# Eight modulation tiles moved from the first layer's FFN to the second layer's front units and mixers

## The chip, the cores and the metric

The kernel runs on one core of one Trainium2 chip. The metric is the device time of the whole program in microseconds (us), the median of several runs. The five engines of a core run their own instruction streams and meet at semaphores: TensorE (PE in the profile; its weight loads are PEld), VectorE (DVE), ScalarE (ACT), GpSimd (POOL) and SyncE (SP, which here only issues DMAs).

## The reference

One inference step of a trunk of two layers, for 128 context tokens and 256 latent tokens with 1024 channels. All is float32. Each layer, for each of the two groups of tokens, computes

```
sh1, sc1, g1, sh2, sc2, g2 = split(silu(c) @ w_mod + b_mod, 6)     # c of the latent group, c_ctx of the context
h   = rmsnorm(x, norm1_g) * (1 + sc1) + sh1
u, q, k, v, z, xbc, dt = split(h @ w_in)
three mixers: pooling of u; differential attention of q, k, v; bidirectional state-space scan of z, xbc, dt
gates = sigmoid(h @ w_gate + b_gate)
x   = x + g1 * ((sum of gate * (mixer @ w_branch)) @ w_out)
h2  = rmsnorm(x, norm2_g) * (1 + sc2) + sh2
up  = dwconv3(h2 @ ffn_w_up);  x = x + g2 * ((silu(up_gate) * up_value) @ ffn_w_down)
```

and a last RMSNorm follows. Context tokens see context tokens only; latent tokens see both. The change is about the first line: the 6 x 1024 values of modulation per layer and group.

## The kernel before

Both groups of tokens go through together as one block of T = 384 columns; activations lie transposed, channels on the 128 partitions. The work of a layer is a fixed list of 140 units (`UNITS`), most of them one tile of 128 output channels: 8 XBC, 4 UU, 4 QQ, 4 KK, 4 VV, 4 ZZ, 24 GATE, 12 BRANCH (two tiles each), 8 OUT, 44 UP, and 24 DOWN (8 tiles in three parts). Each engine walks through the same list in the same order, and its instructions wait for counts that the others reach.

A float32 product is made of three faster ones: weights and activations are split into a high part (rounded to the format fp32r) and a low part. For unit u+3, while unit u is in work (`AHEAD` = 3), ScalarE writes the high part `wh` of the weights (`hi`, L1155), VectorE the low part `wl` (`lo`, L1508), from `raw`, which SyncE loads, 512 KB a unit. TensorE then runs three matmuls for each block: L823, L824, L825. `wh` and `wl` have three buffers each.

The mixers' own work is spread over the units from ZZ to BRANCH: step s is done in unit `MIX0` + s (`MIX0` is the first ZZ, unit 24; GATE 0 is unit 28).

**Modulation.** For one tile of 128 modulation channels, VectorE multiplies a tile of `w_mod` (`rawm`, 512 KB, channels on partitions, two buffers) by a row of silu(c) copied to all partitions, and sums: one `scalar_tensor_tensor` over 1024 columns with `accum_out` for each of the two groups of tokens (L1583, in `modulation`). There are 48 tiles a layer. The first 16 of layer 0 (shift and scale of the first norm) come from a special head; the other 80 are made at units listed by `mod_places`. Tiles go to these places in order. SyncE issues the load of such a tile four units late in its list (`MOD_LEAD`), and waits for the buffer of two tiles before.

The rows of silu(c) lie in `crow`, in memory that the attention needs in the mixers. So they are loaded again (1 MB, by GpSimd's queue) and passed through tanh (ScalarE, `row_tanh`) and silu (VectorE, `rows_silu`) before each FFN. In layer 0 alone they are also loaded into `crow_late` in the midst of the mixers, at unit `LATE_ROWS` - 2 = 31, under gate tiles that are not yet written; the eight units 33 to 40 (`LATE`) make a tile each from it. Those gates (number 13 and on) wait until the last late tile is made.

`summed` adds the bias to ready sums: tiles 0 to 15 of the next layer at `PREP` (unit 134, DOWN unit 18), 16 to 23 at the end of the front units (unit 23), 24 to 39 at `LATE_DONE` (unit 40), 40 to 47 at `G2_LAST`. At `PREP` both VectorE and ScalarE also prepare the next layer's parameters (`params`): VectorE makes `lams`, ScalarE waits for it.

In DOWN, the third part of each tile is followed by an update of `x` (L1720), a square on ScalarE and a running sum of squares on GpSimd (L634).

Of the kernel before, what the change touches and what calls it, by code (L numbers as in the profile page):

```python
# [33 lines left out]
DEPTH = 2  # L34
# [46 lines left out]
MODT = 6 * KT  # L81
MOD_HEAD = 2 * KT
MOD_G2 = 5 * KT
UP0 = U_OF[(UP, 0, 0)]
DOWN0 = U_OF[(DOWN, 0, 0)]
# [12 lines left out]
FRONT = range(UU0, MIX0)  # L98
LATE_ROWS = MIX0 + 9
LATE = range(LATE_ROWS, LATE_ROWS + 8)  # L100
LATE_DONE = LATE[-1]
LATE_TILE = 13
# [25 lines left out]
def mod_places():  # L128

    tiles = [(l, m) for l in range(DEPTH) for m in range(MODT)][MOD_HEAD:]  # L130
    units = [(0, u) for u in FRONT] + [(0, u) for u in LATE]
    units += [(0, UP0 + 3 * i + 4) for i in range(14)] + [(0, DOWN0 + i) for i in range(18)]
    units += [(1, u) for u in FRONT] + [(1, UP0 + 5 * i + 4) for i in range(MODT - MOD_G2)]
    return dict(zip(units, tiles, strict=True))


# [11 lines left out]
MOD_NO = {lu: i for i, lu in enumerate(MODS)}  # L148
# [136 lines left out]
def build(nc, wstream, whead, par, bias, tab, xs, xp, cvec, cvec_rows, kc, vc, st0, fng, y, newk, newv, news):  # L285
    ctx = ExitStack()
    with ctx:
# [28 lines left out]
        with ExitStack() as a:  # L316
            junk_front = sb("junk_front", [P, 2, D], where=a)
# [131 lines left out]
        mod_used = sem("mod_used")  # L449
# [169 lines left out]
        def _(pool):  # L619
# [73 lines left out]
            for l in range(DEPTH):  # L693

                if l:
                    pool.wait_ge(mod_used, sum(lu[0] < l for lu in MODS))
                else:
                    pool.wait_ge(h_lo, SP_N1 + KT)
                load_cache(l)
                for u in range(NU):  # L700
                    if u == OUT0:

                        pool.wait_ge(mod_used, sum(lu < (l, UP0) for lu in MODS))
                        pool.wait_ge(st_out, 32 * (l + 1))
                        pool.wait_ge(gb_done, count(l, 24, 23))
                        pool.dma_start(crow[:, :, :], cvec_rows).then_inc(crow_in, 16)
                    if u + AHEAD in POOL_LO:
                        lo(l, u + AHEAD)
                    if u == 4:
                        clear_pads(l)  # L710
                    if u in POOLING:
                        pooling(l, POOLING.index(u))
                    if u == MIX0 + 8:
                        pool.wait_ge(qk_done, count(l, 2 * HEADS, 2 * HEADS - 1))
                        pool.dma_start(newk[l], kt_[:, :, PAST + CTX0:PAST + T]).then_inc(k_out, 16)
                        pool.wait_ge(v_in, count(l, NCH, NCH - 1))
                        pool.dma_start(newv[l], vv[:, 3, :]).then_inc(v_out, 16)
                    if u == MIX0 + NATT + 2:
                        pool.wait_ge(av_done, count(l, NATT, NATT - 1))
                        pool.wait_ge(k_out, 16 * (l + 1))  # L720
                        pool.wait_ge(v_out, 16 * (l + 1))
                        for d in range(2):
                            pool.dma_start(hst[:, d, :], st0[l, d]).then_inc(state_in, 16)
                    if u in (MIX0 + SLOT_S + 2, MIX0 + SLOT_S + 3):
                        k = u - MIX0 - SLOT_S - 2
                        pool.wait_ge(st_done, count(l, 4, 2 + k))
                        pool.dma_start(news[l, k], end_state[k]).then_inc(st_out, 16)
                    if BRANCH0 + 5 <= u < BRANCH0 + 9:
                        for j in (2 * (u - BRANCH0 - 5), 2 * (u - BRANCH0 - 5) + 1):

                            pool.wait_ge(gb_done, count(l, 24, KT + j))
                            nc.gpsimd.tensor_tensor(gates[:, j, :], gates[:, j, :], gates[:, KT + j, :], ALU.add) \
                                .then_inc(mg_done, 1)
                    if (l, u) == (0, LATE_ROWS - 2):

                        pool.wait_ge(qk_done, count(l, 2 * HEADS, 2 * HEADS - 1))
                        pool.wait_ge(op_done, count(l, 4, 3))
                        pool.dma_start(crow_late[:, :, :], cvec_rows).then_inc(crow_in, 16)
                    if OUT0 <= u < UP0:
                        if u == OUT0:  # L740

                            pool.wait_ge(misc_done, count(l, NMISC, 0))
                        sum_square(u - OUT0, norm_number(l, 1))
                    if u == DOWN0 + 2 and l + 1 < DEPTH:
                        pool.wait_ge(h_full, count(l, NFULL, NFULL - 1))
                        load_params(l + 1)
                    if u >= DOWN0 and UNITS[u][2] == 2:
                        if u == DOWN0 + 2:

                            pool.wait_ge(misc_done, count(l, NMISC, M_N2))  # L750
                        sum_square(UNITS[u][1], norm_number(l + 1, 0))
# [391 lines left out]
        def _(act):  # L1143
# [102 lines left out]
            def row_tanh(n, rows, junk):  # L1246

                act.wait_ge(crow_in, 16 * n)
                for v in range(2):
                    af(junk[:, v, :], rows[:, v, :], ACT.Tanh, scale=0.5).then_inc(crow_tanh, 1)  # L1250
# [9 lines left out]
            def evac(l, g):  # L1260
                kind, j = GROUPS[g]
                bank = acc[g % BANKS]
                group_done(act, l, g)
                if kind in (XBC, UP):
                    n = j if kind == XBC else 8 + j
                    w, b = ("cw", "cb") if kind == XBC else ("fw", "fb")
                    b_ = j % 2
                    tile = j if kind == XBC else (j // 2 + FT * (j % 2))
                    if kind == XBC and j < 2 or kind == UP and j < 2:

                        act.wait_ge(h_lo, count(l, NSPLIT, (SP_N1 if kind == XBC else SP_N2) + KT - 1))
                    elif kind == UP and b_ == 1:
                        act.wait_ge(h_lo, count(l, NSPLIT, SP_FF + j // 2 - 1))
                    else:
                        act.wait_ge(cv_out, count(l, 8 + FT, j - 2 if kind == XBC else 8 + j // 2 - 1))
                    af(cv[:, b_, :], bank[:, 0:T], ACT.Identity, bias=prm_(b, tile), scale=prm_(w, 3 * tile + 1)) \  # L1276
                        .then_inc(cv_init, 1)
                elif kind == UU:

                    act.wait_ge(pads, l + 1)  # L1280
                    af(ut[:, j, ULAT:ULAT + LAT], bank[:, 0:LAT], ACT.Copy)
                    af(ut[:, j, UCTX:UCTX + SEQ], bank[:, CTX0:T], ACT.Copy).then_inc(u_in, 1)
                elif kind in (QQ, KK):
                    dst = qt[:, j, :] if kind == QQ else kt_[:, j, PAST:PAST + T]
                    af(dst, bank[:, 0:T], ACT.Copy).then_inc(qk_in, 1)
                elif kind == VV:
                    af(vv[:, 1 + j, :], bank[:, :], ACT.Copy).then_inc(v_in, 1)
                elif kind == ZZ:
                    if j < 2:

                        act.wait_ge(cv_out, count(l, 8 + FT, 7))
                    else:
                        act.wait_ge(z_done, count(l, 4, j - 2))
                    af(th[:, j % 2, :], bank[:, 0:T], ACT.Tanh, scale=0.5).then_inc(z_tanh, 1)
                elif kind == GATE:
                    if j >= 16:

                        act.wait_ge(op_done, count(l, 4, 3))
                    if l == 0 and j >= LATE_TILE:

                        act.wait_ge(mod_used, MOD_NO[0, LATE[-1]] + 1)
                    af(gates[:, j, :], bank[:, 0:T], ACT.Tanh, bias=bgh[:, j:j + 1], scale=0.5).then_inc(g_done, 1)  # L1302

            def conv_silu(l, g):
# [121 lines left out]
            for l in range(DEPTH):  # L1426
# [14 lines left out]
                for u in range(NU):  # L1441
# [1 line left out]
                        inv_rms(l, M_N2, D)  # L1443
                        norm(l, 1)
                    if u == ROWS_FFN:
                        row_tanh(l + 2, crow, junk_front)
                    if u == PREP and l + 1 < DEPTH:
                        params(l + 1)
                    if UNITS[u] in ((OUT, 4, 0), (DOWN, 4, 2)):
# [25 lines left out]
                    if MIX0 <= u <= MIX0 + SLOT_RMS + 1:  # L1475
# [12 lines left out]
                        if s == SLOT_RMS + 1:  # L1488
                            for i in range(4):
                                act.wait_ge(zn_done, count(l, 4, i))  # L1490
                                high(l, None, osh[:, i, :], zz[:, i, :])
                    if (l, u) == (0, LATE_ROWS - 1):
                        row_tanh(1, crow_late, junk_late)
            inv_rms(DEPTH, 0, D)


# [1 line left out]
        def _(dve):  # L1498
# [422 lines left out]
            for l in range(DEPTH):  # L1921
# [22 lines left out]
                for u in range(NU):  # L1944
# [39 lines left out]
                        mixers_b(l, u - MIX0)  # L1984
                    if last_update:
                        ahead(l, u)
                    if (l, u) == (0, LATE_ROWS - 1):
                        rows_silu(1, crow_late, junk_late)
                    if u == ROWS_FFN:
                        rows_silu(l + 2, crow, junk_front)  # L1990
                    modulation(l, u)
                    if u == MIX0 - 1:

# [137 lines left out]
```

## Time and profile before

| | |
|---|---|
| median of 3 runs | 1383.5 us (1382.97 to 1384.87) |
| the profiled execution | 1383.34 us, its span 1381.6 us |
| TensorE, its weight loads | busy 95%, 90% of the span |
| VectorE | busy 79% |
| ScalarE, GpSimd | busy 47%, 12% |
| mean granted clock of TensorE | 0.991 |
| HBM read | 203.97 MB |

How to read it: the span is from the first to the last instruction of the program, and the run's time has 1.74 us more around it. Busy shares are averages over stages that differ. A matmul's end is modelled, so that TensorE's busy share says little about how close a stage is to its best.

### The profile page before, as it was taken

How to read it: one execution, taken by the hardware profiler on the slowest of the kernel's cores; microseconds unless marked ns; L12 is line 12 of the kernel's file. 1: busy time of each engine (PE TensorE's matmuls, PEld its weight loads, DVE VectorE, ACT ScalarE, POOL GpSimd, SP SyncE). 2: the span in 40 equal slices, each digit the busy share in tenths (PEclk: the TensorE clock that was granted, in tenths of full speed). 3: DMA queues.
4: the chain of work that ended last, by engine and by line, in shares of the span. 5: the costliest groups of instructions: out<-in, count | busy, mean ns of one | idle time of the engine just before them, and what ended most of it. 6: DMA issues, size and time to landing. Idle time of an engine off the chain costs nothing.

```text
span 1381.6 us, 20127 instructions
## 1 busy us (share of the span) xinstructions
PE 1313.4 (95%) x7564; PEld 1243.7 (90%) x7564; DVE 1093.5 (79%) x2102; ACT 646.8 (47%) x1035; POOL 162.6 (12%) x166
## 2 busy tenths in 40 slices
PE   5899999999999999999989999999999899999996
PEld 4799889999988999999979988898999799999996
DVE  5889988679857999999967998637877699989432
ACT  4643445644556444442355335445445654454331
POOL 0058000000210000000100930000031000000001
PEclk8999999999999999999999999999999999999998
DMA  9456535323343454447734572333224244454431
GB/s 361 142 203 209 195 107 198 139 96 104 111 147 100 160 168 152 153 160 258 258 134 153 206 249 79 107 107 107 84 101 152 89 155 143 147 168 132 140 126 46
DMA packets 58289, 208.95 MB, mean 151 GB/s; under 512 B 6736, under 2 KB 8912, under 8 KB 56784
## 3 DMA queue, kind: packets, MB, share of 16 engines
q1 hardware_dynamic: 55648, 197.53, 42.7%
q0 software_dynamic: 2544, 10.13, 2.2%
q8 instruction: 60, 0.98, 0.3%
q14 instruction: 37, 0.30, 0.1%
HBM read 203.97 MB, written 3.67 MB: 150 GB/s over the span
## 4 chain that ended last, share of the span: by engine, by line
PE 44%; DVE 37%; issue 8%; ACT 8%; DMA 1%; POOL 0%; SPq 0%; DVEq 0%; ACTq 0%; POOLq 0%
PE acc L823 12%; PE acc L825 12%; PE acc L824 12%; DVE wl L1508 8%; DVE cv L1658 6%; DVE junk_front L1583 5%; DVE junk_ffn L1583 5%; ACT wh L1155 1%; DVE gates L1702 1%; DVE cv L1679 1%; PE mix L1075 1%; DVE al L1513 1%; ACT ah L1172 1%; DVE x L1720 1%; PE mix L980 1%
## 5 line engine op out<-in xcount | busy, mean ns | idle before, releaser
L823 PE MATMUL acc<-hh,wh 128*128 128x384 f32 x1528 | 524.1, 343 | 14.3 <-DVE wl L1508 11.6
L825 PE MATMUL acc<-hh,wl 128*128 128x384 f32 x1528 | 511.3, 335 | 0.0
L824 PE MATMUL acc<-hl,wh 128*128 128x384 f32 x1528 | 511.1, 334 | 0.0
L1508 DVE TENSOR_TENSOR wl<-raw,wh 128x1024 fp32r<-128x1024 f32 (+1 forms) x280 | 344.8, 1233 | 126.1 <-ACT wh L1155 124.4
L1155 ACT ACTIVATE wh<-raw 128x1024 fp32r<-128x1024 f32 (+1 forms) x280 | 290.7, 1041 | 111.2 <-PE acc L825 110.2
L823 PEld LDWEIGHTS acc<-hh,wh 128*128 128x128 f32 x1528 | 286.8, 188 | 35.0 <-DVE wl L1508 20.9
L824 PEld LDWEIGHTS acc<-hl,wh 128*128 128x128 f32 x1528 | 287.0, 188 | 2.4
L825 PEld LDWEIGHTS acc<-hh,wl 128*128 128x128 f32 x1528 | 286.8, 188 | 0.0
L1658 DVE SCALAR_TENSOR_TENSOR cv<-acc,prm,cv 128x1 f32<-128x1 f32 (+1 forms) x416 | 153.7, 412 | 11.3 <-ACT cv L1276 4.2
L823 PE MATMUL acc<-ah,wh 128*128 128x384 f32 x352 | 119.1, 338 | 3.1 <-DVE wl L1508 2.7
L824 PE MATMUL acc<-al,wh 128*128 128x384 f32 x352 | 118.3, 336 | 0.0
L825 PE MATMUL acc<-ah,wl 128*128 128x384 f32 x352 | 118.2, 336 | 0.0
L1583 DVE SCALAR_TENSOR_TENSOR junk_ffn<-rawm,crow 128x1024 f32<-128x1024 f32 x80 | 99.0, 1275 | 0.0
L1172 ACT ACTIVATE ah<-cv 128x384 fp32r<-128x384 f32 x44 | 23.2, 527 | 139.6 <-DVE cv L1679 139.6
L1583 DVE SCALAR_TENSOR_TENSOR junk_front<-rawm,crow 128x1024 f32<-128x1024 f32 x64 | 87.4, 1401 | 0.0
L823 PEld LDWEIGHTS acc<-ah,wh 128*128 128x128 f32 x352 | 66.5, 189 | 5.4 <-DVE wl L1508 5.4
L1276 ACT ACTIVATE cv<-acc,prm 128x384 f32<-128x384 f32 x104 | 68.6, 659 | 5.6 <-PE acc L825 5.6
L1302 ACT ACTIVATE gates<-acc,bgh 128x384 f32<-128x384 f32 x48 | 28.0, 582 | 83.3 <-PE acc L825 83.3
L825 PEld LDWEIGHTS acc<-ah,wl 128*128 128x128 f32 x352 | 66.6, 189 | 0.0
L824 PEld LDWEIGHTS acc<-al,wh 128*128 128x128 f32 x352 | 66.6, 189 | 0.0
L1314 ACT ACTIVATE th<-cv 128x384 f32<-128x384 f32 x60 | 31.6, 527 | 71.5 <-DVE cv L1658 71.5
L1258 ACT ACTIVATE th<-x 128x384 f32<-128x384 f32 x28 | 14.8, 528 | 81.8 <-DVE x L1720 81.8
(256 smaller groups left out, 1673.1 us busy)
## 6 DMA issues: line engine op xcount, KB each, us to landing
raw<-in_wstream_dram SPq DMA_DIRECT2D x248, 512.0 KB, 3.5
rawm<-in_wstream_dram SPq DMA_DIRECT2D x80, 512.0 KB, 3.8
raw<-in_wstream_dram SPq DMA_DIRECT2D x32, 448.0 KB, 3.3
head<-in_whead_dram SPq DMA_DIRECT2D x8, 1024.0 KB, 14.0
crow<-in_cvec_rows_dram POOLq DMA_DIRECT2D x2, 1024.0 KB, 5.2
out_y_dram<-gates POOLq DMA_DIRECT2D x8, 192.0 KB, 2.7
prm<-in_par_dram POOLq DMA_DIRECT2D x2, 591.5 KB, 4.3
x<-in_xs_dram SPq DMA_DIRECT2D x1, 1024.0 KB, 8.9
```

Of the source, the lines that this page charges most:

```text
L823: mm(out, sh, mhi, start=start, stop=False)
L824: mm(out, sh, mlo, start=False, stop=False)
L825: return mm(out, sl, mhi, start=False, stop=stop)
L1155: af(wh[:, s, 0:n], raw[:, raw_slot(u), 0:n], ACT.Copy).then_inc(hi_done, 1)
L1172: af(dst, src, ACT.Copy).then_inc(h_hi, 1)
L1258: af(th[:, j % 2, :], x[:, j, :], ACT.Square).then_inc(sq_done, 1)
L1276: af(cv[:, b_, :], bank[:, 0:T], ACT.Identity, bias=prm_(b, tile), scale=prm_(w, 3 * tile + 1)) \
L1302: af(gates[:, j, :], bank[:, 0:T], ACT.Tanh, bias=bgh[:, j:j + 1], scale=0.5).then_inc(g_done, 1)
L1314: af(th[:, b_, :], cv[:, b_, :], ACT.Tanh).then_inc(cv_tanh, 1)
L1508: tt(wl[:, s, 0:n], raw[:, raw_slot(u), 0:n], wh[:, s, 0:n].bitcast(F32), ALU.subtract).then_inc(lo_done, 1)
L1583: last = stt(out=junk[:, v, :], in0=rawm[:, n % NMOD, :], scalar=1.0, in1=rows[:, v, :], op0=ALU.mult, op1=ALU.mult, accum_out=macc[:, m, ...
L1658: return stt(out=out, in0=src, scalar=prm_(w, 3 * tile + i), in1=out, op0=ALU.mult, op1=ALU.add)
```

## The change

`mod_places` gives both layers the same pattern. Each layer makes a tile at each of its 16 front units (UU to VV), at the eight late units 33 to 40, and at every fifth UP unit (eight). In layer 0's DOWN, 16 of the first 18 units make one each, all but units 8 and 17. So layer 0's FFN makes 24 tiles where it made 32 (14 at every third UP unit, 18 in DOWN), and layer 1 makes 32 where it made 24. The tiles keep their order: layer 0's FFN stops after tile 15 of layer 1 instead of tile 23, layer 1's front units make tiles 16 to 31, and its late units 32 to 39.

For that, the load of `crow_late`, its tanh and silu, and the wait of the gate tiles from 13 on are now there in both layers.

```diff
 def mod_places():
     tiles = [(l, m) for l in range(DEPTH) for m in range(MODT)][MOD_HEAD:]
-    units = [(0, u) for u in FRONT] + [(0, u) for u in LATE]
-    units += [(0, UP0 + 3 * i + 4) for i in range(14)] + [(0, DOWN0 + i) for i in range(18)]
-    units += [(1, u) for u in FRONT] + [(1, UP0 + 5 * i + 4) for i in range(MODT - MOD_G2)]
+    units = []
+    for l in range(DEPTH):
+        units += [(l, u) for u in FRONT] + [(l, u) for u in LATE]
+        units += [(l, UP0 + 5 * i + 4) for i in range(MODT - MOD_G2)]
+        if l + 1 < DEPTH:
+            units += [(l, DOWN0 + i) for i in range(MOD_HEAD + 2) if i not in (8, 17)]
     return dict(zip(units, tiles, strict=True))
...
-                    if (l, u) == (0, LATE_ROWS - 2):
+                    if u == LATE_ROWS - 2:
                         pool.wait_ge(qk_done, count(l, 2 * HEADS, 2 * HEADS - 1))
                         pool.wait_ge(op_done, count(l, 4, 3))
                         pool.dma_start(crow_late[:, :, :], cvec_rows).then_inc(crow_in, 16)
...
-                    if l == 0 and j >= LATE_TILE:
-                        act.wait_ge(mod_used, MOD_NO[0, LATE[-1]] + 1)
+                    if j >= LATE_TILE:
+                        act.wait_ge(mod_used, MOD_NO[l, LATE[-1]] + 1)
...
                     if u == ROWS_FFN:
-                        row_tanh(l + 2, crow, junk_front)
+                        row_tanh(2 * l + 2, crow, junk_front)
...
-                    if (l, u) == (0, LATE_ROWS - 1):
-                        row_tanh(1, crow_late, junk_late)
+                    if u == LATE_ROWS - 1:
+                        row_tanh(2 * l + 1, crow_late, junk_late)
...
-                    if (l, u) == (0, LATE_ROWS - 1):
-                        rows_silu(1, crow_late, junk_late)
+                    if u == LATE_ROWS - 1:
+                        rows_silu(2 * l + 1, crow_late, junk_late)
                     if u == ROWS_FFN:
-                        rows_silu(l + 2, crow, junk_front)
+                        rows_silu(2 * l + 2, crow, junk_front)
```

## Rows read from the trace of the kernel before

**Rows 1.** The page: span, and busy time by engine.
```profile
span 1381.6 us, 20127 instructions
...
PE 1313.4 (95%) x7564; PEld 1243.7 (90%) x7564; DVE 1093.5 (79%) x2102; ACT 646.8 (47%) x1035; POOL 162.6 (12%) x166
```

**Rows 2.** Windows: UP and DOWN of each layer; length, busy by engine, clock, DMA.
```profile
429.90:613.25 183.35, 175.94 (x985) 169.97 (x985) 167.78 (x324) 83.63 (x123) 0.00 (x0) 1.00 0.47 157
613.25:711.50 98.25, 95.17 (x529) 93.16 (x530) 87.83 (x140) 32.53 (x45) 9.58 (x9) 0.98 0.70 233
...
1102.86:1275.75 172.89, 171.93 (x984) 170.56 (x985) 156.74 (x305) 84.53 (x125) 0.00 (x0) 1.00 0.46 149
1275.75:1367.44 91.69, 91.69 (x530) 91.69 (x530) 35.10 (x49) 29.23 (x35) 5.59 (x6) 1.00 0.33 105
```

**Rows 3.** Waits: layer 0's UP, its DOWN, layer 1's UP (us, times, longest).
```profile
PEld acc L823 <- DVE wl L1508: 14.1, 22, 1.5
...
PEld acc L823 <- DVE wl L1508: 5.4, 7, 2.6
...
PEld acc L823 <- DVE wl L1508: 3.0, 6, 1.2
```

**Rows 4.** Timeline where DOWN begins, layer 0 and layer 1: start, us, instruction.
```profile
611.98 1.22 DVE L1508 TENSOR_TENSOR wl<-raw,wh 128x1024 fp32r<-128x1024 f32 x1
613.25 0.44 PE L823 MATMUL acc<-ah,wh 128*128 128x384 f32 x1
...
1273.17 1.22 DVE L1508 TENSOR_TENSOR wl<-raw,wh 128x1024 fp32r<-128x1024 f32 x1
1275.75 0.33 PE L823 MATMUL acc<-ah,wh 128*128 128x384 f32 x1
```

**Rows 5.** Groups by line: modulation passes in UP of layer 0, of layer 1.
```profile
L1583 DVE SCALAR_TENSOR_TENSOR junk_ffn<-rawm,crow 128x1024 f32<-128x1024 f32 x26 | 30.8, 1222 | 0.0
...
L1583 DVE SCALAR_TENSOR_TENSOR junk_ffn<-rawm,crow 128x1024 f32<-128x1024 f32 x16 | 18.9, 1221 | 0.0
```

**Rows 6.** Timeline in DOWN: layer 0, then layer 1.
```profile
655.40 0.73 DVE L1720 SCALAR_TENSOR_TENSOR x<-acc,mod,x 128x256 f32<-128x256 f32 x2
...
656.77 1.36 POOL L634 TENSOR_TENSOR sqa<-sqa,th 128x384 f32<-128x384 f32 x1 [10.48 <-ACT th L1258]
...
657.19 2.03 DVE L1583 SCALAR_TENSOR_TENSOR junk_ffn<-rawm,crow 128x1024 f32<-128x1024 f32 x1
...
667.24 0.73 DVE L1720 SCALAR_TENSOR_TENSOR x<-acc,mod,x 128x256 f32<-128x256 f32 x2
...
1292.70 1.23 DVE L1508 TENSOR_TENSOR wl<-raw,wh 128x1024 fp32r<-128x1024 f32 x1 [2.52 <-ACT wh L1155]
...
1304.15 1.23 DVE L1508 TENSOR_TENSOR wl<-raw,wh 128x1024 fp32r<-128x1024 f32 x1 [2.52 <-ACT wh L1155]
```

**Rows 7.** Timeline at `PREP` of layer 0; in brackets the idle time before.
```profile
690.94 0.73 DVE L1720 SCALAR_TENSOR_TENSOR x<-acc,mod,x 128x256 f32<-128x256 f32 x2
...
694.81 0.29 DVE L1630 TENSOR_TENSOR lamt<-prm 128x128 f32<-128x128 f32 x1
...
695.45 0.21 ACT L1244 ACTIVATE lams<-lams 128x2 f32<-128x2 f32 x1 [2.91 <-DVE lams L1631]
...
698.20 0.58 PE L823 MATMUL acc<-ah,wh 128*128 128x384 f32 x1 [2.24 <-DVE wl L1508]
```

**Rows 8.** Windows: behind that idle time; the granted clock is third from the end.
```profile
698.40:701.70 3.30, 3.30 (x11) 3.30 (x11) 2.40 (x4) 0.86 (x3) 0.00 (x0) 0.50 0.62 204
```

**Rows 9.** Windows: from the first ZZ to the first OUT, layer 0 and layer 1.
```profile
146.36:374.33 227.97, 225.49 (x1379) 207.05 (x1378) 188.88 (x423) 117.52 (x208) 15.04 (x15) 1.00 0.39 130
820.17:1047.34 227.17, 225.23 (x1379) 207.06 (x1378) 167.89 (x389) 115.61 (x206) 14.46 (x14) 1.00 0.33 107
```

**Rows 10.** Late passes of layer 0 (ns min/median/max, us), and the timeline at `crow_late`.
```profile
L1583 DVE SCALAR_TENSOR_TENSOR junk_late<-rawm,crow_late x16: 1218/1222/1226, 216.9 to 253.8; 128x1024 f32<-128x1024 f32 x16
...
209.08 2.01 ACT L1250 ACTIVATE junk_late<-crow_late 128x1024 f32<-128x1024 f32 x2 [0.50 <-DMA crow_late<-in_cvec_rows_dram]
```

## The prediction

> **What bounds the kernel now.** I read the page first: TensorE is busy for 95% of the span, VectorE for 79% [rows 1]. That average hides that both layers run the same units with a different spread of modulation tiles, so the second layer is a measured sample of what the change makes of the first, and the other way round. I therefore cut the span at the same units in both layers (the k-th matmul of the trace gives the unit, since the order is fixed) and compared.
>
> From unit (UP, 3) to the first DOWN unit the first layer takes 183.35 us and the second 172.89; the 24 DOWN units take 98.25 against 91.69 [rows 2]. TensorE has exactly the same matmuls in both. The reader is to see VectorE's column: it is busy for 167.78 us of the first UP stretch and 87.83 of the first DOWN stretch, but for 156.74 and 35.10 in the second layer. The view of waits names the link: a weight load on TensorE waits for `wl`, the low part of the weights, which VectorE writes at L1508: 14.1 us in the first layer's UP and 5.4 in its DOWN, against 3.0 in the second layer's UP [rows 3] (in the second layer's DOWN TensorE is busy for all 91.69 us). VectorE is one in-order engine, and each modulation tile sits on it between one `wl` and the next. So in the first layer's FFN VectorE sets the pace (183.35 / 41 = 4.47 us a unit), and in the second layer's nearly always TensorE does (172.89 / 41 = 4.22).
>
> **The first layer's UP.** The change makes 8 tiles at every fifth unit where there were 14 at every third. That is the second layer's list, unit for unit. The stretch held 26 passes of `junk_ffn` in the first layer and 16 in the second [rows 5], that is 13 and 8 tiles; a tile is two passes of 1.22 us, some 2.4 us. Five tiles less are 12 us of VectorE; what of it was on the path is the difference of the two stretches, 183.35 - 172.89 = 10.46 us. The bounds are 0 and 12; I take 10.46, as a row of the very sequence that will run. (The last of the 14 tiles was at the last UP unit, and slowed DOWN.) `summed` of the last eight tiles, one small op, comes at a later unit; it is first read by DOWN's updates of `x`, behind it on VectorE.
>
> **The first layer's DOWN.** Eighteen units with a tile become sixteen, and units 8 and 17, the third parts of their groups, are free. While VectorE sets the pace, one group of three units repeats every 11.84 us (the update of `x` at 655.40 and at 667.24), whereas in the second layer the first `wl` of a group comes at 1292.70 and 1304.15, every 11.45 us, and VectorE waited 2.52 us for ScalarE before each [rows 6]. So VectorE lacks 0.40 us a group. Before, it came to DOWN with nothing in hand: `wl` ended at 613.20 and TensorE took it at 613.25. In the second layer it ended at 1274.39 for 1275.75, 1.36 us ahead [rows 4], and no tile follows until unit 0 of DOWN. Two full groups lose 0.8 of the 1.36. The third has a unit without a tile and gets 2.4 us or more back; three groups more lose little of that, and the sixth is again one tile short. By this count TensorE never waits in DOWN.
>
> At one place it mattered most. At `PREP` (DOWN unit 18) ScalarE and VectorE prepare the next layer's parameters. VectorE updated `x` at 690.94, ran the tile of unit 17, and only at 694.81 began on `lams`, for which ScalarE stood 2.91 us until 695.45 with the next `wh` behind it. TensorE idled 2.24 us until 698.20 [rows 7], and in the 3.30 us from 698.40 its clock was 0.50, that is 1.2 GHz, which costs another 1.7 [rows 8]. With unit 17 free and VectorE not behind, `lams` comes some 3 us sooner and the idle goes, and with it the fall of the clock, as the second layer's DOWN has neither. I take the whole difference, 98.25 - 91.69 = 6.56 us; the bounds are 0 and 6.56.
>
> What stands beside the tile matters too: one pass of each group took 2.03 us instead of 1.22, beside GpSimd's sum of squares of 1.36 at 656.77 [rows 6]. The Trainium skill, GPSIMD Engine Reference, section Specifications, says that GpSimd shares its SBUF interface with VectorE, against instructions with two SBUF inputs; the trace agrees with 2.03 against 1.22. By that rule the freed unit's `wl` would be stretched in the tile's place, and the free unit would give 2.4 us and not 3.2; by the row alone 3.2; neither changes the sum, as both leave VectorE ahead.
>
> **The second layer's front.** 16 tiles at the same units as before, other columns. Nothing changes; the sums taken at its end are over tiles made by then in both.
>
> **The second layer's mixers.** New here: one DMA of 1 MB for `crow_late` on GpSimd's queue, two ScalarE tanh, two VectorE silu, eight tiles (16 passes), their eight DMAs of 512 KB on SP's queue, the `scale_of` for norm 2 (already there), and a wait before each gate tanh from number 13 for the last late tile. The first layer does exactly all this. Between the same units (first ZZ to first OUT) it takes 227.97 us and the second 227.17, with VectorE at 188.88 and 167.89 [rows 9]. So 21.0 us more of VectorE work cost 0.80 us. The cover is the stage's chain of attention and scan, in which VectorE has gaps: without it the cost is the whole 21.0. The 0.80 arises where ScalarE waits 0.50 us for `crow_late`, then runs two tanh (2.01 us) ahead of a gate and of `wh` [rows 10]. All 16 late passes lie between 216.9 and 253.8 us and take 1218 to 1226 ns [rows 10], so nothing of GpSimd's stretches them. The gate wait names a tile that is made in the unit before the first gate that waits; behind it in ScalarE's queue are `wh` for three units on and the scan's copies, for which TensorE and VectorE wait; what it costs is inside the first layer's 227.97 too. On GpSimd the cache outputs are queued behind the new DMA, which waits only for VectorE's rotation and the pooled outputs, as before. On SP's queue the eight loads stand among the `raw` loads just as in the first layer. I take 0.80, with bounds 0 and 21.0.
>
> **Sum.** -10.46 - 6.56 + 0.80 = -16.22 us. The profiled execution took 1383.34 us, 1.74 of it around the span of 1381.6; the three runs shown have the median 1383.5, 0.16 above it. From the span: 1365.4; with what lies around it 1367.1; against the median 1367.3. I predict 1367.2.
>
> **Rivals.**
> DOWN stays at VectorE's pace. Sixteen of eighteen tiles are still there, and VectorE is 0.40 us a group short; the small lead may be lost, for instance if GpSimd's sum of squares falls on more passes. Against it: the lead and the two free units. If the idle and the clock fall at `PREP` stay (2.24 + 1.7), the time is 1367.2 + 3.9 = 1371.1; if all 6.56 stay, 1373.8. Chance 0.09.
>
> The mixers do not hide it (slower). The place is the second layer's mixers: if there the 21.0 us of VectorE work stood on the path, the sum would be -17.02 + 21.0 = +4.0, 1387.5 us; it decides above 17.0 of the 21.0. For it: VectorE would be busy for 189 of 228 us there. Against it: the first layer hides 20.2 of the 21.0 with the same order of work. Chance 0.03.
>
> TensorE bounds the FFN anyway. With 95% busy it might be that the first layer's stretches are long for another cause, such as the clock or the traffic, and the time stays at 1383.5. For it: TensorE shows 95.17 us busy of the 98.25. Against it: a granted clock of 1.00 in the UP stretch and a named wait for `wl` [rows 2, 3]. The Trainium skill, Perfetto Trace Analysis, section Identifying the Most-Contended Engine, says to find the engine of highest occupancy and optimize it first; taken over the whole span that is TensorE, and lighter VectorE work would be worth nothing (1383.5); taken stage by stage, as its next section allows, it does not decide. Chance 0.03.
>
> A fall of the clock at another place. The stages shift in time, and another of TensorE's idle times, at a norm or in the mixers, might bring a spell at 1.2 GHz like that one: +1.7, 1368.9. Against it: of the stretches shown only the first layer's DOWN is below 1.00 [rows 2, 9]. Chance 0.07, inside the likeliest one's range.
>
> **How the numbers follow.** The likeliest, 0.78, is 1367.2, and its own range is 1365.5 to 1369.5: the cost of the mixers between 0 and 2, one spell more, and the spread of the runs (2 us). The range of 8 in 10 takes this and a part of the first rival: 1365.0 to 1371.2. About 0.2% (2.8 us) is what a measurement of this kernel can tell from no change. Faster holds the likeliest, the clock and the DOWN rival: 0.94; same 0.03; slower 0.03.
>
> **What would show it.** The UP stretch of the first layer near 172.9 us, with 16 passes of `junk_ffn`; DOWN near 91.7 with no wait for `wl` and the clock at 1.00; the second layer's mixers near 228.0 with 16 `junk_late` passes of 1.22 us and a wait of 0.5 us for `crow_late`; everything else unchanged but shifted. Wrong would make it: a DOWN of 95 or more, mixers above 230, or a wait of ScalarE before gate 13.

## The result, and the profile after

The changed kernel takes 1368.65 us (median of 4 runs, 1367.94 to 1369.37) against 1384.18 for the kernel before in the same series. The ratio is 0.9889, with a 95% interval of 0.9872 to 0.9906: 15.5 us less, where 16.2 were forecast. The profiled execution took 1367.94 us, its span is 1366.2.

The page of the changed kernel, to be read against [rows 1]:

```profile
span 1366.2 us, 20140 instructions
...
PE 1308.7 (96%) x7564; PEld 1245.6 (91%) x7564; DVE 1095.0 (80%) x2104; ACT 647.9 (47%) x1037; POOL 162.3 (12%) x167
```

VectorE is as busy as before, 1.5 us more in all: the two extra silu passes add 2.4, and two passes fewer are stretched to 2.03 us beside GpSimd. The work was moved, not removed. The windows of the changed kernel, cut at the same units as [rows 2] and [rows 9] (length, busy by engine, granted clock, DMA share, GB/s); in order the first layer's UP and its DOWN, the second layer's mixers and its UP, and at last the piece from the end of DOWN to the fourth XBC unit of the second layer:

```profile
428.76:601.61 172.85, 171.93 (x985) 170.54 (x986) 156.81 (x305) 84.33 (x125) 0.00 (x0) 1.00 0.47 149
601.61:693.29 91.68, 91.68 (x530) 91.68 (x530) 79.47 (x127) 32.31 (x44) 8.84 (x9) 1.00 0.70 237
804.16:1032.01 227.85, 225.47 (x1379) 207.04 (x1378) 188.71 (x423) 117.32 (x208) 15.01 (x15) 1.00 0.40 130
1087.46:1260.31 172.85, 171.93 (x985) 170.54 (x986) 156.81 (x305) 84.33 (x125) 0.00 (x0) 1.00 0.46 149
...
693.29:714.27 20.98, 17.62 (x79) 15.83 (x78) 12.16 (x25) 14.97 (x28) 0.27 (x3) 0.84 0.16 50
```

The same last piece in the kernel before:

```profile
711.50:730.33 18.83, 15.22 (x79) 13.11 (x78) 12.16 (x25) 15.03 (x28) 0.27 (x3) 1.00 0.16 55
```

The reader is to see three things. The first layer's UP (172.85) is now the second layer's UP to the digit. The first DOWN, 91.68 us, has TensorE busy for every one of them, while VectorE is busy for 79.47 of the 91.68: it is nearly full and yet sets nothing. And the piece behind DOWN, in which no instruction was changed, is 2.15 us longer, at a granted clock of 0.84 instead of 1.00.

From these the difference of the two profiled spans, 15.4 us, adds up: UP -10.50, DOWN -6.57, the second mixers +0.68, the piece behind DOWN +2.15, everything ahead of the first UP -1.14 (0.90 of it ahead of the first ZZ, in instructions that the change does not touch), the rest within 0.1. So the three stages that were forecast at -16.22 gave -16.39. The 2.15 behind DOWN was not forecast, and that the head took half of it back is luck.

The wait at `PREP` of [rows 7] in the changed kernel, ScalarE's and then VectorE's timeline:

```profile
675.94 0.19 ACT L1247 ACTIVATE lams<-lams 128x2 f32<-128x2 f32 x1
676.04 1.05 ACT L1158 ACTIVATE wh<-raw 128x1024 fp32r<-128x1024 f32 x1
...
674.43 0.74 DVE L1723 SCALAR_TENSOR_TENSOR x<-acc,mod,x 128x256 f32<-128x256 f32 x2
675.09 0.28 DVE L1633 TENSOR_TENSOR lamt<-prm 128x128 f32<-128x128 f32 x1
```

`lamt` begins 0.66 us after the update of `x` began, where it was 3.87 us in [rows 7]; the bracket with ScalarE's 2.91 us is gone.

The clock. In the windows, the clock of a stretch stands third from the end. Outside the program's head and its last norm the changed kernel's profile has one spell at half clock. It lies at the second layer's first norm:

```profile
697.60:704.10 6.50, 5.66 (x18) 5.69 (x19) 5.81 (x14) 6.41 (x15) 0.00 (x0) 0.50 0.17 61
```

Ahead of it TensorE did little but the sum of squares, and waited (its timeline, in brackets the idle time before):

```profile
694.79 0.91 PE L778 MATMUL misc<-th,tb 128*128 128x384 f32 x2 [0.21 <-DVE th L1730]
698.45 0.66 PE L922 MATMUL acc<-hh,wh 128*128 128x384 f32 x1 [2.74 <-ACT hh L1224]
```

So the spell behind the wait at `PREP` [rows 8] is gone, and another one, at least 6.5 us long, has come at a place that had none. That is the part of the forecast to examine.

### The profile page after: what moved, and what is told of

Same layout as the page of the kernel before. It is cut to its first block, busy times and chain, and to the rows that moved or that the text cites. A ratio compares the mean times of both kernels' runs of the same rounds, so it can differ in the third digit from the quotient of the medians.

```text
span 1366.2 us, 20140 instructions
## 1 busy us (share of the span) xinstructions
PE 1308.7 (96%) x7564; PEld 1245.6 (91%) x7564; DVE 1095.0 (80%) x2104; ACT 647.9 (47%) x1037; POOL 162.3 (12%) x167
## 4 chain that ended last, share of the span: by engine, by line
PE 60%; DVE 26%; ACT 7%; issue 5%; DMA 1%; POOL 0%; SPq 0%; ACTq 0%; DVEq 0%; POOLq 0%
PE acc L826 17%; PE acc L827 17%; PE acc L828 17%; DVE wl L1511 6%; DVE junk_front L1586 5%; DVE cv L1661 3%; ACT wh L1158 1%; DVE gates L1705 1%; PE mix L1078 1%; DVE ee L1796 1%; DVE ee L1785 1%; PE mix L983 1%; DMA head<-in_whead_dram 1%; DVE hl L1516 1%; DVE x L1723 1%
## 5 line engine op out<-in xcount | busy, mean ns | idle before, releaser
L1586 DVE SCALAR_TENSOR_TENSOR junk_ffn<-rawm,crow 128x1024 f32<-128x1024 f32 x64 | 78.4, 1263 | 0.0
L826 PE MATMUL acc<-mh,wh 128*128 128x384 f32 x128 | 43.0, 336 | 3.1 <-DVE ml L1516 3.1
```

What stands on the lines that cost most here:

```text
L826: mm(out, sh, mhi, start=start, stop=False)
L1586: last = stt(out=junk[:, v, :], in0=rawm[:, n % NMOD, :], scalar=1.0, in1=rows[:, v, :], op0=ALU.mult, op1=ALU.mult, accum_out=macc[:, m, ...
```

## The experiments

**First series: the parts.** Each run undoes one part of the changed kernel. The kernel before had a median of 1384.02 us there.

*18 tiles in DOWN.*

```diff
-            units += [(l, DOWN0 + i) for i in range(MOD_HEAD + 2) if i not in (8, 17)]
+            units += [(l, DOWN0 + i) for i in range(MOD_HEAD + 2)]
...
-        units += [(l, u) for u in FRONT] + [(l, u) for u in LATE]
+        units += [(l, u) for u in FRONT] + [(l, u) for u in LATES[l]]   # layer 1: the first 6 of LATE
```

> The changed kernel, but the first layer's DOWN makes a tile at each of its first 18 units again and the second layer's mixers make six late tiles. Theory (VectorE's lead): UP stays at 172.85 us. VectorE comes to DOWN 1.36 us ahead and then loses 0.40 us in each of six groups, 2.4 us in all, so that TensorE waits about 1.0 us before the parameters of the next layer, and there about 2 us more, as before the change: DOWN 94.7 us against the changed kernel's 91.68, total about 1371.5. Rival (the lighter UP alone cures DOWN, the two free units are worth nothing): DOWN 91.7 and the changed kernel's 1368.65. Clock: if the half clock follows TensorE's idle time, it comes behind the wait at the parameters; if it sticks to the time since the clock last rose, it comes at 697 to 698 us whatever TensorE does there.

Measured: 1370.95 us, ratio 0.9910 (0.9892 to 0.9928). The windows (UP, DOWN) and the two rows at `PREP`:

```profile
428.99:601.84 172.85, 171.90 (x984) 170.52 (x985) 156.76 (x305) 84.38 (x125) 0.00 (x0) 1.00 0.46 149
601.84:695.41 93.57, 91.99 (x530) 91.67 (x530) 84.89 (x135) 32.32 (x44) 9.72 (x9) 1.00 0.74 244
```

```profile
680.93 0.20 ACT L1248 ACTIVATE lams<-lams 128x2 f32<-128x2 f32 x1 [2.91 <-DVE lams L1635]
...
683.67 0.44 PE L827 MATMUL acc<-ah,wh 128*128 128x384 f32 x1 [1.58 <-DVE wl L1512]
```

Half a hit. The wait at `PREP` is back, ScalarE's with the same 2.91 us as before and TensorE's with 1.58. But it is TensorE's only wait in DOWN; the 1.0 us that I expected ahead of it did not come. In the windows of DOWN the whole 93.57 - 91.68 = 1.89 us is that place. TensorE's clock stayed at 1.00 behind these 1.58 us. Its spells in this profile lie at the first layer's second norm and at the second layer's first.

The 1.0 us did not come because VectorE's lead was larger than I counted. The lead is the time from the end of a unit's `wl` (its start and length added) to TensorE's first matmul of the same unit. These are the two rows for DOWN unit 6, and then for unit 18:

```profile
620.91 1.23 DVE L1512 TENSOR_TENSOR wl<-raw,wh 128x1024 fp32r<-128x1024 f32 x1
624.72 0.33 PE L827 MATMUL acc<-ah,wh 128*128 128x384 f32 x1
...
668.43 1.23 DVE L1512 TENSOR_TENSOR wl<-raw,wh 128x1024 fp32r<-128x1024 f32 x1
670.48 0.33 PE L827 MATMUL acc<-ah,wh 128*128 128x384 f32 x1
```

That is 2.6 us at unit 6 and 0.8 at unit 18, a loss of 0.44 a group. The same reading gives 1.4 at unit 0, so in the first two groups VectorE gains.

*14 tiles in UP, as before.*

```diff
-        units += [(l, UP0 + 5 * i + 4) for i in range(MODT - MOD_G2)]
+            units += [(l, UP0 + 3 * i + 4) for i in range(14)]            # layer 0
...
+        units += [(l, u) for u in LATES[l]]                               # layer 1: the first 2 of LATE
```

> The changed kernel, but the first layer's UP makes 14 tiles at every third unit as before, DOWN keeps its 16, and the second layer's mixers make only two late tiles. Theory: UP is 183.35 us again. DOWN starts without a lead, waits about 1 us in the first two groups, and the free units 8 and 17 remove the wait at the parameters: about 92.8 us. Total 1368.65 + 10.5 + 1.1 = 1380.3. Rival (UP's gain was only work pushed into DOWN, so that the sum of both stretches counts): DOWN nearer to 98 and 1385. A second rival (VectorE's total load of the FFN counts, not its place): 6 tiles of 2.4 us, 14.4 us, 1383.

Measured: 1379.75 us, ratio 0.9974 (0.9959 to 0.9988). UP and DOWN:

```profile
429.06:612.31 183.25, 175.78 (x985) 169.89 (x985) 167.74 (x324) 83.50 (x123) 0.00 (x0) 1.00 0.48 158
612.31:705.23 92.92, 92.41 (x529) 91.71 (x530) 82.39 (x132) 32.60 (x45) 8.84 (x9) 1.00 0.71 235
```

A hit at both: 183.25 and 92.92 against 183.35 and 92.8. Of the six more tiles in UP, five lie in this stretch and cost 10.4 us there; the sixth is at the last UP unit, and coming to DOWN without a lead costs 1.24. The two effects are separate.

This run also answers what I asked of the clock in the run before. The second layer's first norm comes later here, with its joint units (the first three units behind a norm, which TensorE does together) starting at 710.39 instead of 700.56, and the spell moved with it. First the run with 18 tiles, then this one:

```profile
701.80:705.00 3.20, 3.20 (x12) 3.20 (x11) 2.92 (x7) 3.10 (x8) 0.00 (x0) 0.50 0.01 4
```

```profile
711.90:715.10 3.20, 3.20 (x11) 3.20 (x11) 2.68 (x6) 3.13 (x7) 0.00 (x0) 0.50 0.00 0
```

*The late rows without the late tiles.* The second layer's late tiles and the wait of its gates for them are left out, and their sums are zero, so this kernel and the next do not compute the reference.

```diff
+    tiles = [t for t in tiles if t not in [(1, m) for m in range(32, 40)]]
...
+                    if (l, u) == (1, LATE_ROWS - 1):
+                        step.then(nc.vector.memset(macc[:, 32:40, :], 0.0))
```

> The changed kernel without the second layer's late tiles 32 to 39 (their sums are set to zero, so shift, scale of norm 2 there are only the bias); the rows crow_late are still loaded, passed through tanh and silu. Theory: the mixers' 0.68 us is all of the rows (two tanh and two silu ahead of others), the eight tiles are hidden: second layer's mixers 227.8 us, total within 0.3 us of the changed kernel. Rival: the tiles make the 0.68: total 0.7 us less.

Measured: 1368.41 us. *Neither the rows nor the tiles:* the same, and the load, tanh and silu of `crow_late` only in layer 0.

> The changed kernel without the second layer's late tiles and without their rows (sums set to zero as in the run with rows only). Theory: the second layer's mixers fall to the 227.17 us of before, total 0.7 us less than the changed kernel. Rival: nothing, since the first ZZ to OUT stretch is set by attention and scan alone: equal. Clock: this kernel is the changed one up to the second layer's mixers, so a spell at half clock at 697.5 us should be there again if it is no accident.

Measured: 1368.45 us. Medians cannot tell 0.7 us here, so the windows of the second layer's mixers must. First the kernel with rows only, then the one with neither:

```profile
803.61:1030.94 227.33, 225.25 (x1379) 207.01 (x1378) 170.30 (x392) 117.31 (x208) 15.02 (x15) 1.00 0.35 112
```

```profile
802.72:1030.56 227.84, 225.28 (x1380) 207.04 (x1379) 168.59 (x392) 115.54 (x206) 14.44 (x14) 1.00 0.34 108
...
DVE junk_front L1587 <- DMA rawm<-in_wstream_dram: 0.5, 1, 0.5
```

With rows only, 227.33 stands 0.16 above the 227.17 of [rows 9], and the changed kernel 0.52 above that. My expectation is refuted: the tiles make most of the 0.68, the rows little. The kernel with neither does not show the expected 227.17. Its last row, from the view of waits, says why: in this one execution the load of a front tile's `rawm` landed 0.5 us late, and the first two ZZ steps were 0.66 us longer. From there on it keeps the pace of the kernel before. It is a miss that says nothing on the late tiles. Of the clock it says something: up to the second layer's mixers this is the changed kernel, and the spell at the second layer's first norm is there again, but shorter (its joint units take 14.44 us at 0.90, in the changed kernel 15.82), with another one at the first layer's second norm, where the changed kernel's profile has none.

Where the 0.52 arises is to be seen in VectorE's timeline in step 9 of the mixers, first the kernel before, then the changed one:

```profile
892.19 0.56 DVE L1732 TENSOR_REDUCE mxb<-mix 128x1 f32<-128x384 f32 x1 [1.49 <-PE mix L980]
```

```profile
874.60 1.22 DVE L1586 SCALAR_TENSOR_TENSOR junk_late<-rawm,crow_late 128x1024 f32<-128x1024 f32 x1
...
875.74 1.22 DVE L1586 SCALAR_TENSOR_TENSOR junk_late<-rawm,crow_late 128x1024 f32<-128x1024 f32 x1
...
877.00 0.56 DVE L1735 TENSOR_REDUCE mxb<-mix 128x1 f32<-128x384 f32 x1
```

Ahead of the maximum of the next scores VectorE had 1.49 us free; a tile takes 2.4 and starts into the same gap. It overruns it by some 0.9, on the chain score, maximum, exponential. The following late tiles cost nothing more: the run with 14 tiles in UP makes only two late tiles in the second layer, and its mixers take 227.90 us. The 0.16 of the rows is hardly above what the same mixers differ by from one profile to the next (227.07 and 227.17 in two profiles without rows and tiles). The first gates from 13 on waited for no `mod_used` that the trace shows.

**Second series: which unit counts, and two ways further.** The kernel before had 1385.17 us there.

*17 tiles in DOWN, unit 17 alone free; seven late tiles.*

```diff
-            units += [(l, DOWN0 + i) for i in range(MOD_HEAD + 2) if i not in (8, 17)]
+            units += [(l, DOWN0 + i) for i in range(MOD_HEAD + 1)]
```

> The changed kernel, but the first layer's DOWN makes 17 tiles, at its first 17 units: unit 8 gets its tile back, unit 17 stays free, and the second layer's mixers make seven late tiles. The run with 18 tiles in DOWN lost 0 us up to the parameters of the next layer and 1.9 us there. Theory (only the tile just ahead of the parameters is on a path, since it stands before the product that ScalarE waits for): DOWN 91.7 us as in the changed kernel. Rival (the lead that unit 8 gives back is needed later on): 92.5 or more, as in between the 91.68 with 16 tiles and the 93.57 with 18.

Measured: 1369.42 us, ratio 0.9896 (0.9873 to 0.9919). DOWN:

```profile
601.68:693.36 91.68, 91.68 (x530) 91.68 (x530) 82.44 (x131) 32.16 (x44) 9.19 (x9) 1.00 0.72 243
```

91.68, as with 16 tiles. The tile at unit 8 costs nothing; the one at unit 17 is worth 1.89 us.

*The second layer's last eight tiles in its DOWN.*

```diff
-        units += [(l, UP0 + 5 * i + 4) for i in range(MODT - MOD_G2)]     # now in layer 0 only
+        else:
+            units += [(l, DOWN0 + 3 * j) for j in range(MODT - MOD_G2)]
...
+                    if l + 1 == DEPTH and (l, u) in MOD_NO and u >= DOWN0:
+                        j = UNITS[u][1]
+                        summed(l, MOD_G2 + j, MOD_G2 + j + 1)
```

> The changed kernel, with the second layer's tiles 40 to 47 (the gate of the FFN) made in its DOWN, one at the first part of each group of three, instead of in its UP; each is added up at once. Theory: that DOWN has VectorE busy for 35 of 91.7 us, so eight tiles (19.5 us) hide there and it stays 91.7. UP, 172.85 us with 16 passes, stands above 41 units at TensorE's own pace (41 x 4.16 = 170.6); the first tile, at the second unit of the stretch, is where VectorE is still behind from the norm, so UP falls by 0.5 to 2.2 us. Total 0.5 to 2.2 us less than the changed kernel. Rival: the 2.3 us at the start of UP come from the three joint units, which free the weight buffers late, and not from tiles: UP stays 172.85 and the total is the same.

Measured: 1368.13 us, ratio 0.9880 (0.9863 to 0.9897). The second layer's UP:

```profile
1087.88:1259.87 171.99, 171.12 (x984) 170.61 (x985) 142.53 (x278) 87.70 (x127) 0.00 (x0) 1.00 0.42 131
```

0.86 us less than 172.85, and its DOWN was unchanged. Within the expected span, at its low end: most of what UP has above TensorE's own pace is not the tiles'.

*TensorE kept busy at the norms.* Four float32 matmuls that nobody reads (the filling) stand behind the sum of squares at three norms, where TensorE otherwise waits.

```diff
+            def keep_busy():
+                for _ in range(4):
+                    mm(mix7[:, 0:T], ones, tb[:, 0:T], start=True, stop=True)
...
                     mean_squares(l, 0)          # and after mean_squares(l, M_N2)
+                    keep_busy()
```

> The changed kernel, with four more float32 matmuls of 384 columns (on tables that lie ready, into a bank that nobody reads) behind each layer's second sum of squares and behind the second layer's first one, where TensorE otherwise waits 2.7 us for the first normalised tile. Theory (the half clock comes behind TensorE's idle time at the norms): it no longer falls at the norms, the mean granted clock goes up by 0.001 to 0.003, and the median is 1 to 3 us below the changed kernel's 1368.65, with less spread. Rival (the fall has to do with something else, or so little filling does not count): clock and time as before; if the four matmuls take longer than the wait that they fill, up to 0.5 us later at each of three places.

Measured: 1365.55 us, ratio 0.9863 (0.9846 to 0.9880). TensorE's timeline at the first layer's second norm, and the window from the first XBC unit of the second layer to the fourth:

```profile
412.23 2.74 PE L783 MATMUL mix<-tb 128*128 128x384 f32 x8
415.13 0.41 PE L927 MATMUL acc<-hh,wh 128*128 128x384 f32 x1 [0.16 <-ACT hh L1231]
```

```profile
698.42:712.05 13.63, 13.01 (x73) 12.38 (x73) 8.19 (x18) 11.88 (x23) 0.00 (x0) 1.00 0.01 5
```

The filling takes 2.74 us in place of the 2.74 us wait, of which 0.16 is left. It delays nothing: the joint units start at 415.13 us, in the changed kernel at 415.16. The joint units take 13.63 us at clock 1.00, against 14.4 to 15.9 us with clocks of 0.90 to 0.81 in the kernels without filling of the first two series. In this profile the clock is at 1.00 from the program's head to its final norm. The timed runs have granted clocks of 0.990 to 0.992, the changed kernel's 0.987 to 0.989. The changed kernel did not run in this series; the two runs that differ least from it, with 17 tiles and with the last tiles in DOWN, took 1369.42 and 1368.13 us there.

*Both.*

> Both edits: the tiles 40 to 47 of the second layer in its DOWN, and the four filling matmuls at three norms. Theory: they add up, 1.5 to 5 us below the changed kernel, 1364 to 1367 us. Rival: as for the two alone, the changed kernel's 1368.65.

Measured: 1364.36 us (1363.77 to 1364.81), ratio 0.9854 (0.9834 to 0.9874), as expected.

**Third series: side by side.** The kernel before had 1384.15 us there (17 runs).

*The kernel before with the same filling.*

> The kernel before the change, with the four filling matmuls at the same three norms. It separates the clock at the norms from the clock at the parameters of the next layer, where TensorE idles 2.24 us. Theory (a fall follows TensorE's idle time wherever that is): a spell at half clock behind the wait at the parameters is still there in the profile or in a part of the runs, none at the norms; the time is 1 to 3 us below the kernel before, and the changed kernel with the same filling (1365.55) is 16.0 to 18 us below this one. Rival (the fall at the parameters was the same thing as the one at the norms): no spell in the span's middle and 16 us or less.

Measured: 1380.55 us, ratio 0.9968 (0.9957 to 0.9979). DOWN, and TensorE at `PREP`:

```profile
612.00:708.64 96.64, 93.55 (x529) 91.54 (x530) 87.82 (x140) 32.48 (x45) 9.59 (x9) 1.00 0.71 237
```

```profile
696.92 0.45 PE L828 MATMUL acc<-ah,wh 128*128 128x384 f32 x1 [2.23 <-DVE wl L1515]
```

The same idle time as in [rows 7], 2.23 us, and this time no fall of the clock behind it. DOWN is 96.64 instead of 98.25, so the fall had cost 1.6. The expectation (a spell still there in the profile or in a part of the runs) is not borne out by this profile, nor do the 12 timed runs hint at it, with granted clocks of 0.990 to 0.994. And the two kernels with filling are 1380.55 - 1365.55 = 15.0 us apart, below the 16 to 18 expected; by their spans 1378.5 - 1364.1 = 14.4, by the two ratios (0.9863 / 0.9968) 14.6. Both signs are the rival's: no spell in the middle, and less than 16 us.

*The changed kernel again.*

> The changed kernel once more, so that it stands on one chip beside the two with filling. Expected 15.0 to 16.5 us below the kernel before, spells at half clock at the norms as in its other profiles, and runs that spread by 1.5 us or more.

Measured: 1369.76 us, ratio 0.9902 (0.9882 to 0.9923), 14.4 us below the kernel before, a little less than the 15.0 to 16.5 expected. Its runs spread from 1368.26 to 1376.78. The longest was the profiled one, and its mixers show why:

```profile
819.60:829.60 10.00, 9.65 (x31) 8.21 (x32) 7.87 (x22) 1.99 (x6) 0.00 (x0) 0.50 0.28 95
```

Ten us at half clock, and a wait ahead of them, make the window from the first ZZ to the first OUT 235.30 us instead of 227.85. First two rows of its waits (us, times, longest), all of them between 790 and 820 us, and the matmul at which the spell begins; then the same matmul in the first profile of the changed kernel, whose waits have neither row:

```profile
ACT wh L1158 <- DMA raw<-in_wstream_dram: 8.4, 3, 3.8
DVE junk_front L1586 <- DMA rawm<-in_wstream_dram: 2.7, 3, 1.1
...
819.95 0.90 PE L997 MATMUL mix<-tb,pr 128*128 128x128 f32 x3 [3.25 <-DVE pr L1748]
```

```profile
816.72 0.55 PE L997 MATMUL mix<-tb,pr 128*128 128x128 f32 x3 [0.29 <-DVE pr L1748]
```

Loads of `raw` and `rawm` landed late, VectorE came late with `pr`, and TensorE stood 3.25 us instead of 0.29; the clock fell at the end of that wait. Counted from the first ZZ, this matmul is 3.0 us late, and the other 4.5 of the 7.45 us are added in the spell. Why the loads were late in this execution, no run shows.

*Both edits again.*

> Both edits once more beside the changed kernel: expected 3 to 5 us below it on the same chip, no spell at half clock between 60 and 1350 us, and a spread of about 1 us. Rival (the 4.3 us between them came from different chips): 1 us or less.

Measured: 1365.09 us (1363.53 to 1366.23), ratio 0.9862 (0.9844 to 0.9880): 4.7 us below the changed kernel in the same series and on the same chip, so that the 4.3 us between the series was no matter of chips. This version beats both kernels. It computes all of the reference; the filling matmuls are in addition.

## Why the prediction was right, and where it was off

*What bounds the kernel.* Right. The second layer's UP was a true sample: forecast 172.89, measured 172.85. Undoing the UP part alone brought 183.25 back. It was VectorE's work at that place, not TensorE's busy share nor the traffic: DMA moves 237 GB/s in the new DOWN, as much as in the old one with its 233 [rows 2], and TensorE waits for nothing there.

*DOWN.* The sum was right (6.56 forecast, 6.57 measured), the account of it was not in two steps. First, "two full groups lose 0.8 of the 1.36" and the credit of the third: the run with 18 tiles loses 0.44 a group, about what I counted, but from a lead of 2.6 us at unit 6 and not of 1.36 at unit 0, and still has 0.8 at unit 18. So TensorE waits nowhere ahead of `PREP`, with or without the free unit 8, and unit 8 was worth nothing (the run with 17 tiles). My own row at [rows 4] was read too early: `wl` is made three units ahead, and between that row and the first DOWN tile VectorE has units without a tile and gains on TensorE. Second, "with it the fall of the clock": see below.

*The stall at `PREP`.* Right, and shown by four runs: a tile at unit 17 gives ScalarE its 2.91 us of wait for `lams` (18 tiles), no tile there gives none (16 and 17 tiles, and 14 in UP). Its price depends on VectorE's lead: 1.58 us of TensorE's time with a lighter UP, 2.24 without. The freed `wl` was not what GpSimd's sum of squares met: in the changed kernel a small product of the parameters, 128 x 24, took 1.00 us instead of 0.30 beside it, and hid; neither of the two ways in which I counted the free unit changed the sum.

*The mixers.* The size was right (0.80 forecast, 0.68 measured), the place wrong: not "ScalarE waits 0.50 us for `crow_late`, then runs two tanh" (0.16 with rows only) but the first late tile, which does not fit into the gap ahead of a maximum.

*The clock.* This is the step that failed: that 1.7 us of DOWN's difference go for good with the idle time at `PREP`. In the kernel before with filling, the same idle time of 2.23 us had no fall behind it, and the changed kernel got 2.15 us of the like at the next norm, which the forecast had as unchanged. Without the 1.7, the sum is -10.46 - 4.86 + 0.80 = -14.5 us. That is what the two kernels with filling differ by (14.4 in the spans, 14.6 by the ratios), and the two plain comparisons gave 15.5 and 14.4. By this account the forecast of 1367.2 should have been 1369.0; measured were 1368.65 and 1369.76. The rival "a fall of the clock at another place" named the event and its size (+1.7), but I gave it 0.07; of the eight profiles taken after the change without filling (the changed kernel twice, and the runs with 18 tiles, 14 tiles, rows only, neither, 17 tiles and the last tiles in DOWN) all show a spell at the second layer's first norm, six another at the first layer's second norm, and three (neither, the last tiles in DOWN, the changed kernel the second time) one at the second layer's second norm. At the second layer's first norm a spell makes the joint units 0.8 to 2.3 us longer than the 13.6 without one.

*The rivals.* DOWN at VectorE's pace: no, TensorE is busy 91.68 of 91.68. Mixers exposed: no, 0.68 of 21.0. TensorE bounds the FFN anyway: no.

*What stays open.* All four profiles with filling have no spell between the head and the final norm, so as far as four profiles show, the falls at the norms need TensorE's idle time there. Why one execution falls at a norm and another not, with the same instructions and the same idle time, no run shows. The kernel before fell at neither norm in its profile, and its medians with and without filling are still 3.6 us apart, so its other executions probably had spells that were not profiled; their granted clocks in the third series, 0.984 to 0.989 against 0.991 in the profile, say the same. The fall at `PREP` is known from a single profile, and its absence there with filling from another. Nothing was tried against the late loads and the spell in the mixers of the repeated run.

## What to carry to other kernels

When two passes of a loop run the same instructions with a different load beside them, cut the trace at the same units: the difference of the stretches prices the load to a tenth of a microsecond, where busy shares only say that an engine is 80% full. Background work on an in-order engine costs by what stands right behind it: 1.9 us ahead of a value that another engine waits for, nothing nine units earlier where the engine still has a lead, 0.5 us where the gap is 1.5 and the piece 2.4 us. Do not credit an edit with a fall of the clock seen once in one profile; compare the granted clocks of all runs first, and fill TensorE's short waits if they matter.

## What the runs showed of the hardware

The granted clock goes with most of the spread of one kernel's runs. The kernel before ran from 1382.12 us at 0.988 to 1388.37 at 0.984, and the changed one from 1368.26 at 0.988 to 1376.78 at 0.984 (there 3.0 us are a wait ahead of the spell). I had not expected that 2.74 us of idle ahead of the joint units, with little but the sum of squares before it, would in some executions bring TensorE down to 1.2 GHz and in others not, nor that twelve useless matmul calls would make the kernel before 3.6 us faster (1384.15 to 1380.55). The Trainium skill, TensorE: Matmul & The Clock Gate, section Why this matters for your kernels, advises against long idle gaps of TensorE between bursts of matmuls, because the clock drops back behind them. The trace agrees in the mixers, where 3.25 us of idle ended in a granted clock of 0.50, and at the norms, with 0.50 in the changed kernel and 1.00 once the 2.74 us were filled; at `PREP` the same 2.2 us were followed by a fall once and not the other time.
